# Sums of the norms by quarters of the tokens, roots on a quarter of the columns, and the heads' norms side by side

## What is computed

```python
def rmsnorm_3(x, g):
    x32 = x.astype(jnp.float32)
    y = x32 * lax.rsqrt(jnp.mean(x32 * x32, axis=-1, keepdims=True) + EPS)
    return (y * g.astype(jnp.float32)).astype(x.dtype)
...
    ml_out = jax.nn.sigmoid(ml_o.astype(f32)) * head_rmsnorm(ml_h, ml_norm_w, ML_HEADS)
```

## Time and profile before

| | |
|---|---|
| median of 3 runs | 3986.44 us (3984.21 to 3989.53) |
| the profiled execution | 3983.62 us, its span 3981.8 us, granted clock of PE 0.918 |
| PE busy | 3481.9 us (87%) |
| DVE, ACT, POOL busy | 1792.2, 1161.9, 974.5 us |
| norms | 20 of 512 columns, 4 of 264, 2 of 256, 1 of 16 |

### The profile page before, as it was taken

One profiled execution on the slowest core, in us unless ns is written; L12 is line 12 of the kernel. 1 busy time (PEld: TensorE's weight loads), 2 busy tenths in 40 slices (PEclk: granted clock), 3 DMA queues, 4 the chain that ended last, 5 costly groups with the idle time before them and its releaser, 6 DMA issues. The chain is left out here.

```text
span 3981.8 us, 40388 instructions
## 1 busy us (share of the span) xinstructions
PE 3481.9 (87%) x16055; PEld 2713.5 (68%) x16055; DVE 1792.2 (45%) x2748; ACT 1161.9 (29%) x1835; POOL 974.5 (24%) x414
## 2 busy tenths in 40 slices
PE   4999978998999799999897777799998835799998
PEld 3887735865888588888786653278887713467886
DVE  5994566654331323456207856522202088442211
ACT  2232323324442321121421133233223214443222
POOL 0001301432444122323220001034442300013443
PEclk8999988999999899999997778699998957699999
DMA  4222402451323123334210010022331200012332
GB/s 169 95 96 90 150 30 99 163 174 50 99 93 97 54 85 101 132 136 146 68 59 6 1 43 6 16 77 99 95 95 60 76 0 14 0 43 80 96 97 83
DMA packets 91047, 315.87 MB, mean 79 GB/s; under 512 B 10726, under 2 KB 12518, under 8 KB 89962
## 3 DMA queue, kind: packets, MB, share of 16 engines
q1 hardware_dynamic: 88492, 304.90, 23.4%
q10 hardware_dynamic: 2368, 8.39, 0.6%
HBM read 311.16 MB, written 2.10 MB: 79 GB/s over the span
## 5 line engine op out<-in xcount | busy, mean ns | idle before, releaser
L239 POOL TENSOR_TENSOR terms<-streams,terms 128x1024 fp32r<-128x1024 f32 (+2 forms) x410 | 974.3, 2377 | 2981.4 <-ACT terms L227 2981.4
L444 PE MATMUL bank<-terms,terms 128*128 128x512 f32 (+2 forms) x4096 | 1521.1, 371 | 127.3 <-DVE terms L650 58.5
L445 PE MATMUL bank<-terms,terms 128*128 128x512 f32 (+2 forms) x4096 | 1513.7, 370 | 0.0
L446 PE MATMUL bank<-terms,terms 128*128 128x512 f32 (+2 forms) x4096 | 1511.7, 369 | 0.0
L227 ACT ACTIVATE terms<-streams 128x1024 fp32r<-128x1024 f32 (+1 forms) x462 | 475.6, 1030 | 1818.6 <-PE bank L446 1658.6
L444 PEld LDWEIGHTS bank<-terms,terms 128*128 128x128 f32 x4096 | 780.1, 190 | 285.4 <-issue 133.4
L446 PEld LDWEIGHTS bank<-terms,terms 128*128 128x128 f32 x4096 | 780.5, 191 | 128.8
L445 PEld LDWEIGHTS bank<-terms,terms 128*128 128x128 f32 x4096 | 781.6, 191 | 122.8
L1403 DVE TENSOR_TENSOR stage<-stage,bank 128x256 f32<-128x256 f32 (+1 forms) x88 | 54.6, 622 | 598.6 <-ACT stage L1393 598.6
L910 DVE SCALAR_TENSOR_TENSOR arena<-arena,vec 128x512 f32<-128x512 f32 x240 | 162.5, 745 | 0.2
L598 PE MATMUL bank<-sq,mean 128*128 128x512 f32 (+2 forms) x226 | 108.0, 626 | 54.1 <-ACT sq L615 54.1
(11 more groups left out here) (290 smaller groups left out, 3190.7 us busy)
## 6 DMA issues: line engine op xcount, KB each, us to landing
streams<-in_ffn_w SPq DMA_DIRECT2D x104, 512.0 KB, 3.3
streams<-in_w_mod SPq DMA_DIRECT2D x72, 512.0 KB, 3.4
streams<-in_w_up SPq DMA_DIRECT2D x44, 512.0 KB, 3.2
streams<-in_w_gu SPq DMA_DIRECT2D x44, 512.0 KB, 3.5
streams<-in_w_ada SPq DMA_DIRECT2D x32, 512.0 KB, 3.3
streams<-in_w_down SPq DMA_DIRECT2D x32, 512.0 KB, 3.5
streams<-in_w_v SPq DMA_DIRECT2D x24, 512.0 KB, 3.9
streams<-in_ffn_w SPq DMA_DIRECT2D x24, 384.0 KB, 3.2
```

What stands on the lines that cost most here:

```text
L239: gp.tensor_tensor(self.low(m), self.raw(n), self.high(m), ALU.subtract).then_inc(self.low_made.sem, 1)
L444: pe.matmul(out, high[:, at], x_high, start=kk == start, stop=False)
L445: pe.matmul(out, high[:, at], x_low, start=False, stop=False)
L446: mm = pe.matmul(out, low[:, at], x_high, start=False, stop=kk == kts - 1)
```

## The change

The sum of a tile is taken by four matmuls in place of one (`by_strips`). Each has 32 columns of ones as weights and a quarter of the tokens as its moving side, and writes 32 partitions of the bank: quarter g of the tokens lies on partitions 32g to 32g+31, in the first 128 columns. The root and the reciprocal then work on 128x128. Behind the reciprocal, four matmuls of 128 columns (`widen`) with the matrices `k.strip` (one row of ones, row 32g, the rest zero) bring the quarters back to 128x512 in the same bank, and the products read PSUM instead of `k.rstd`. In a norm with a mean, ACT copies the quartered mean out of PSUM (`averages`), and `widen` spreads it before DVE subtracts. Norms of other widths go the same way with their own quarter (64, 66 or 4 columns).

`HeadNorms` replaces `stage_head_norms`: four heads in four banks and four parts of `k.rstd`, with the product with the gates taken beside. The first one stands inside the pass `MemoryStart` (gates, sums of the heads, first step of the queries, widening, second step), the second one between two `Halves` at the start of the next `run`. Two `run`s and two blocks with their barriers are gone.

```diff
-        self.ones = k.mean[:, mean, :]
+        self.ones = k.mean[:, mean, 0:32]
+        self.strip = n // 4
...
+    def by_strips(self, pe, of, x, start, stop):
+        w = self.strip
+        for g in range(4):
+            mm = pe.matmul(self.k.bank[of[0]][32 * g:32 * g + 32, :w], self.ones, x[:, g * w:(g + 1) * w],
+                           start=start, stop=stop)
+        return mm
+
+    def widen(self, pe, of, x):
+        w = self.strip
+        for g in range(4):
+            mm = pe.matmul(self.k.bank[of[0]][:, g * w:(g + 1) * w], self.k.strip[:, g, :], x, start=True, stop=True)
+        return mm
...
         if self.center:
             self.means_of(pe)
+            self.means_widened(pe)
         self.sums(pe)
+        self.widened(pe)
...
-            mm = pe.matmul(self.bank(self.mean_bank), self.ones, self.src(j), start=j == 0, stop=j == nt - 1)
+            mm = self.by_strips(pe, self.mean_bank, self.src(j), j == 0, j == nt - 1)
         mm.then_inc(k.pe_done.sem, 1)
+
+    def means_widened(self, pe):
+        k = self.k
+        pe.wait_ge(*k.averaged(1))
+        self.widen(pe, self.mean_bank, k.middle[:, :self.strip]).then_inc(k.spread.sem, 1)
...
             pe.wait_ge(*k.act_done(j + 1))
-            pe.matmul(self.bank(self.sum_bank), self.ones, self.squared(j), start=j == 0, stop=j == nt - 1
-                      ).then_inc(k.pe_done.sem, 1)
+            self.by_strips(pe, self.sum_bank, self.squared(j), j == 0, j == nt - 1).then_inc(k.pe_done.sem, 1)
+
+    def widened(self, pe):
+        k = self.k
+        pe.wait_ge(*k.inverted(1))
+        self.widen(pe, self.sum_bank, k.rstd[:, :self.strip]).then_inc(k.widened.sem, 1)
...
+    def averages(self, act):
+        k = self.k
+        act.wait_ge(*k.pe_done(1))
+        if k.spread.base:
+            act.wait_ge(*k.spread(0))
+        act.activation(k.middle[:, :self.strip], k.bank[self.mean_bank[0]][:, :self.strip], ACT.Copy
+                       ).then_inc(k.averaged.sem, 1)
...
-        if k.dve_done.base:
-            act.wait_ge(*k.dve_done(0))
-        act.activation(k.rstd[:, :self.n], self.bank(self.sum_bank), ACT.Sqrt, bias=self.eps
-                       ).then_inc(k.bank_free[self.sum_bank[0]].sem, 1)
+        if k.widened.base:
+            act.wait_ge(*k.widened(0))
+        act.activation(k.rstd[:, :w], k.bank[self.sum_bank[0]][:, :w], ACT.Sqrt, bias=self.eps
+                       ).then_inc(k.rooted.sem, 1)
...
-        dve.wait_ge(*k.pe_done(1))
+        dve.wait_ge(*k.spread(1))
...
+    def inverse(self, dve):
+        k, w = self.k, self.strip
+        dve.wait_ge(*k.rooted(1))
+        dve.reciprocal(k.rstd[:, :w], k.rstd[:, :w]).then_inc(k.inverted.sem, 1)
...
-        dve.wait_ge(k.bank_free[self.sum_bank[0]].sem, self.sum_bank[1] + 1)
-        dve.reciprocal(k.rstd[:, :n], k.rstd[:, :n]).then_inc(k.dve_done.sem, 1)
-        dve.wait_ge(*k.dve_done(self.centred + 1))
+        k, nt = self.k, self.nt
+        rstd = self.bank(self.sum_bank)
+        dve.wait_ge(*k.widened(1))
         for j in range(nt):
             x = self.whole(j) if self.center else self.src(j)
             if self.gain:
-                ins = dve.scalar_tensor_tensor(self.whole(j), x, self.gain(j), k.rstd[:, :n], ALU.mult, ALU.mult)
+                ins = dve.scalar_tensor_tensor(self.whole(j), x, self.gain(j), rstd, ALU.mult, ALU.mult)
...
+        dve.wait_ge(*k.dve_done(self.centred + nt))
+        dve.sem_inc(k.bank_free[self.sum_bank[0]].sem, 1)
...
+class HeadNorms(Pass):
...
+        self.banks = [k.take_bank() for _ in range(heads)]
...
+    def sums(self, pe):
+        k = self.k
+        for h, (b, uses) in enumerate(self.banks):
+            if uses:
+                pe.wait_ge(k.bank_free[b].sem, uses)
+            pe.wait_ge(*k.act_done(h + 1))
+            for g in range(4):
+                mm = pe.matmul(k.bank[b][32 * g:32 * g + 32, :P], k.mean[:, 2, 0:32],
+                               self.squares_at[:, h, g * P:(g + 1) * P], start=True, stop=True)
+            mm.then_inc(k.pe_done.sem, 1)
+
+    def widened(self, pe):
+        k = self.k
+        for h, (b, _) in enumerate(self.banks):
+            pe.wait_ge(*k.inverted(h + 1))
+            for g in range(4):
+                mm = pe.matmul(k.bank[b][:, g * P:(g + 1) * P], k.strip[:, g, :], k.rstd[:, h * P:(h + 1) * P],
+                               start=True, stop=True)
+            mm.then_inc(k.widened.sem, 1)
+
...
+    def roots(self, act):
+        k = self.k
+        if k.widened.base:
+            act.wait_ge(*k.widened(0))
+        for h, (b, _) in enumerate(self.banks):
+            act.wait_ge(*k.pe_done(h + 1))
+            act.activation(k.rstd[:, h * P:(h + 1) * P], k.bank[b][:, :P], ACT.Sqrt, bias=k.eps[:, 1:2]
+                           ).then_inc(k.rooted.sem, 1)
...
+    def inverses(self, dve):
+        k = self.k
+        for h in range(self.heads):
+            dve.wait_ge(*k.rooted(h + 1))
+            r = k.rstd[:, h * P:(h + 1) * P]
+            dve.reciprocal(r, r).then_inc(k.inverted.sem, 1)
...
+    def scaling(self, dve):
+        k = self.k
+        for h, (b, _) in enumerate(self.banks):
+            dve.wait_ge(*k.widened(h + 1))
+            dve.wait_ge(*k.dve_done(h + 1))
+            dve.scalar_tensor_tensor(self.out[:, h, :], self.out[:, h, :], k.v(self.weight, h), k.bank[b][:, :],
+                                     ALU.mult, ALU.mult).then_inc(k.dve_done.sem, 1)
+        for h, (b, _) in enumerate(self.banks):
+            dve.wait_ge(*k.dve_done(self.heads + h + 1))
+            dve.sem_inc(k.bank_free[b].sem, 1)
...
-        self.steps_of = {"pe": [("means", norm.means_of)] * norm.center + [("sums", norm.sums)],
-                         "act": [("squares", norm.squares), ("root", norm.root), ("shifted", norm.shifted)],
-                         "dve": [("centring", norm.centring)] * norm.center + [("scaling", norm.scaling)]}
+        mean = norm.center
+        self.steps_of = {"pe": [("means", norm.means_of), ("means", norm.means_widened)] * mean
+                         + [("sums", norm.sums), ("widened", norm.widened)],
+                         "act": [("means", norm.averages)] * mean
+                         + [("squares", norm.squares), ("root", norm.root), ("shifted", norm.shifted)],
+                         "dve": [("centring", norm.centring)] * mean
+                         + [("inverse", norm.inverse), ("scaling", norm.scaling)]}
...
+        dve.memset(k.strip[:, :, :], 0.0).then_inc(k.constants.sem, 1)
+        dve.wait_ge(*k.constants(5))
+        for g in range(4):
+            dve.memset(k.strip[32 * g:32 * g + 1, g, :], 1.0).then_inc(k.constants.sem, 1)
...
+        self.averages(act)
...
+    def tensor(self, pe):
+        self.gates.tensor(pe)
+        self.heads.sums(pe)
+        self.queries.tensor_step(pe, 0)
+        self.heads.widened(pe)
+        self.queries.tensor_step(pe, 1)
+
+    def scalar(self, act):
+        self.heads.squares(act)
+        self.gates.scalar(act)
+        self.heads.roots(act)
+        self.queries.scalar(act)

     def vector(self, dve):
-        dve.memset(self.k.arena[:, ML_QP:ML_Q], 0.0).then_inc(self.k.dve_done.sem, 1)
+        k, n = self.k, self.heads.heads
+        self.heads.gated(dve)
+        dve.wait_ge(*k.dve_done(n))
+        dve.memset(k.arena[:, ML_QP:ML_Q], 0.0).then_inc(k.more[3].sem, 1)
+        self.gates.vector(dve)
+        self.heads.inverses(dve)
+        self.queries.vector_step(dve, 0)
+        self.heads.scaling(dve)
+        self.queries.vector_step(dve, 1)
...
     passes = before + [SecondGains(k, 16, 0, 16, ((0, 0), (1, 1)), ()),
-                       Beside(k, down_one, ctx1, sums=4, squares=2, root=4, shifted=4, scaling=4), VectorsAgain(k, down_one)]
+                       Beside(k, down_one, ctx1, sums=4, squares=2, root=4, inverse=4, widened=5, shifted=5, scaling=5), VectorsAgain(k, down_one)]
...
-    passes.append(Beside(k, of_queries, ctx2, sums=3, squares=1, root=3, shifted=3, scaling=3))
+    passes.append(Beside(k, of_queries, ctx2, sums=3, squares=1, root=3, inverse=3, widened=4, shifted=4,
+                         scaling=4))
...
-    stage_head_norms(k, k.a(B2_OUT, 4, 512), "hg_norm", k.a(B2_QG + 4 * 512, 4, 512))
     run(k, memory_inputs(k, lat_src, src))
     stage_mlstm(k)
-    stage_head_norms(k, k.a(ML_OUT, 4, 512), "ml_norm", k.a(ML_O, 4, 512))
...
-    halves = Halves(k, lambda j: outs[j], h, DT)
+    first = Halves(k, lambda j: outs[j], h, HEADS2)
+    heads = HeadNorms(k, k.a(ML_OUT, HEADS2, 512), "ml_norm", k.a(ML_O, HEADS2, 512), HEADS2)
+    halves = Halves(k, lambda j: outs[HEADS2 + j], lambda j: h(HEADS2 + j), HEADS2, heads.ready)
...
-    meta = Beside(k, down, meta_norm(k), sums=4, squares=2, root=4, shifted=4, scaling=4)
+    meta = Beside(k, down, meta_norm(k), sums=4, squares=2, root=4, inverse=4, widened=5, shifted=5, scaling=5)
...
-    return [halves, out, third, up, LoadMeta(k), meta, final]
```

(15 more changed lines are left out.)

85 lines of the change are left out of this document (63 added, 22 removed).

## The result

The changed kernel takes 3880.26 us, the median of 4 runs (3876.61 to 3881.37), beside 3985.32 us of the kernel before in the same session: ratio 0.9731, 95% interval 0.972 to 0.9743. The profiled execution has a span of 3878.6 us, 103.2 less.

The account below looks back on a forecast made before the run. PE, busy 87% of the span, bounds the kernel, so time is won where it stands: 32.3 + 13.7 + 7.1 + 2.5 + 2.1 - 0.2 + 20.2 + 14.0 = 91.7 off 3983.62, plus 2.8: 3895 us, range 3880 to 3918.

Parts of the forecast that it names:

- PE's matmuls elsewhere are the same, so nothing gives it back later: Outside the changed stretches: PE's work stays the same, so the summed saving of 91.7 us stays whole.
- the amount added for the median of before: At the end of the sum: 2.8 us, by which the profiled execution before lay under its median of 3986.44.
- The clock rival: In the norms: PE's clock falls at each norm, so 17 widenings take 0.9 more: 15 us, 3910; chance 10%.
- RMS norms: Seven RMS norms of 512 columns: 12.08 us becomes 8.05 in three, others save 4.6 to 6.0; 32.3 saved in all.
- `ln2`: Norm with a mean: ACT's copy stands behind a Silu waiting for a DMA, centring starts 1.3 later; 2.1 us saved.
- Narrow norms and the rest: Norms of 256, 264 and 16 columns: small gains and losses, -0.2 us in all.
- The first heads' stretch: First heads' norms, from mixer through gates' layer to outputs' layer: 20.2 us saved, bounds 17 and 21.
- the 1.8 for a fast start: Gates' layer behind the first mixer: starting in the fast clock saves 1.8 us more.
- Pairs: Sums of the norms: strips run only two at a time, 0.53 us a tile, total 3906; chance 8%.
- strips one behind another: Sums of the norms: each strip waits for its weights, 1.0 us a tile, total 3964; chance 7%.
- The slower side: Sums of the norms: every one of eight records costs full length, 2.2 us a tile, total 4127; chance 3%.
- The gates' stretch: First heads' norms: PE stands at the heads' widening and scans come late, 10 us given back, 3905; chance 7%.

Follow-up runs that it names:

- e8: Changed kernel with the means' matmuls ordered quarter by quarter over all eight tiles, the sums of squares in their old order: 3898.77 us, ratio 0.978.
- e1: Changed kernel without HeadNorms at both places, heads' norms one behind another again, sums by quarters kept: 3922.49 us, ratio 0.9841.
- e2: Changed kernel with class Norm as before (one matmul a tile, 512 columns, no copy or widening), heads side by side kept: 3940.40 us, ratio 0.9886.
- e5: Kernel before, unchanged, for a second trace: 3985.25 us in one execution.
- e7: Kernel before with a block in which DVE clears 1536 columns ahead of the second mixer: 3983.75 us in one execution.
- e9: Changed kernel with unread matmuls: two ahead of and two behind a 512-column norm's sums, four strips behind each tile but the last: 3884.52 us, ratio 0.9741.
- e10: Changed kernel with the vectors' Silu and both waits for it moved behind ln2's root (ACT) and products (DVE): 3876.36 us, ratio 0.9727.
- e3: Changed kernel with the copy of the quartered mean made by DVE in place of ACT: 3882.14 us, ratio 0.9741.
- e4: Changed kernel with unread matmuls: four ahead of and five behind a 512-column norm's sums, one wide one behind each tile but the last: 3933.65 us, ratio 0.9875.
- e6: Kernel before with a block in which DVE clears 512 columns ahead of the second mixer: 3978.39 us in one execution.
- e11: Changed kernel with the edits of e9 and e10 together: 3874.83 us, ratio 0.9714.
- e12: Kernel before with the 512-column clearing block of e6 again, now timed over ten runs: 3975.86 us, ratio 0.9975.

## Why the prediction was wrong

**The bound and the mechanism held.** The time came from PE's stands at norms and heads' norms, and the prices of the single operations stand in the trace after: a tile by strips 0.24 (64 records in 1.95, forecast 0.27), squares 0.52 and 0.60, root 0.37, reciprocal 0.95, the widening 1.16 where the clock was fast (forecast 1.06). e8 shows that the strips really run side by side, e1 and e2 that the two parts are worth some 42 and 60 us with what the clock adds.

**The step that failed** is "PE's matmuls elsewhere are the same, so nothing gives it back later". It put the clock elsewhere at nothing: the same matmuls at another time may be granted another clock. The second mixer took 9.9 us less with the same 330 records, all of it in PE's busy time. It shows four lengths in fourteen traces, and each comes again to 0.1 us: 112.9 (before, e5, e8), 110.5 (e1, e7), 105.0 (e2, e9, e10), 103.0 (after, e3, e4, e6, e11, e12). The first negations already tell them apart: the third comes 21.75, 20.92, 21.69 and 21.34 us behind the first. Shift the kernel before by one short block and it gets the 103.0 of the changed one (e6, e12). Against such a kernel before, 3975.9 us, the change is worth 95.6 us, and 91.7 were summed. The range had no term for this, of either sign. Of the 14.7 us between 3895 and 3880.3 the stretches make 11.5, of which the mixer is 9.9; 2.8 are the amount added for the median of before, which had no counterpart after (profiled 3880.42, median 3880.26); the rest is rounding.

**The clock rival came true,** though the total does not show it. It had 10% and 15 us; 11 of 17 widenings ran slow, ten of them at 0.9 more, 10 us in all. The forecast counted on a fast clock because the sums of the earlier trace rows kept it; those sums filled PE, under the new ones it was busy 0.84 and 0.81 of the two stretches around the fall. e9, which fills their rounds, keeps 1.00 over the sums and takes the slow widening away in eight of the eleven places.

**Mis-sized terms.** RMS norms: 28.0 for 32.3; four of their seven widenings ran slow (3.7), the fast ones took 1.16 for 1.06, and the forecast's 8.05 is itself 0.14 too low in three of the norms, since 12.08 less 2.35, 0.32 and 2.40, with 1.06 and 0.12 added, is 8.19. `ln2`: the step "the copy stands on ACT behind the Silu" named only half; DVE's program waits for the same Silu (e3), and with the slow widening nothing was left of 2.1. Narrow norms and the rest: -0.2 became 6.5. The sums of the two context norms stand inside dense layers, on PE's own path, and these stretches are 1.5 and 2.3 shorter. The attention is 2.1 shorter: its four narrow norms became 1.2 longer (four widenings of 1.98 each), and the piece behind them went from 133.5 to 130.5 us, at a granted clock of 0.81 against 0.78. The other 0.6 is spread over places without an edit. The first heads' stretch: 21.7 for 20.2, just over its bound of 21. The gates' layer started at a granted clock of 0.50 as before, so the 1.8 for a fast start was not there; the outputs' layer and `w_out2` got such a start instead (1.4 and 1.8). PE was not made late by the heads' widening (0.9 expected), and the part ahead of the scans grew by 1.6 where 2.7 was expected. Without the mixer the terms sum to 93.4 for 91.7, since the slow widenings and these gains cancel.

**Range and rivals.** Pairs, and strips one behind another, are out (0.24 a tile). The slower side is out by the same number. The gates' stretch gave nothing back beyond its terms.

**Open:** what fixes the moments at which the chip lowers or raises the clock; the runs show only that in this mixer they repeat with the program and jump with a shift of 1 to 2 us. No run gave the changed kernel a slow mixer with nothing else altered; e8 has it with the means altered too.

## What to carry to other kernels

A stretch in which PE is nearly the bound, has short pauses and shows a mean granted clock between 0.5 and 1 may have several lengths, as this mixer has, and an edit ahead of it may throw it into another: give the forecast a term for it, and before you credit an edit with a gain, compare the untouched stretches one by one. A delay block in the kernel before is a cheap test. Sums over partitions of few distinct results are cheaper by column strips, if neighbours in PE's program use different strips and the shape of the weights changes seldom. When a norm gets lighter for PE, the matmul that ends it may run at half the clock.

## What the hardware showed that was not expected

The same mixer, same instructions, ran in 112.9, 110.5, 105.0 or 103.0 us, and a delay of about 1 us made the whole kernel 10 us faster (0.9975). A change between weights of 32 and of 128 columns cost about 0.14 us, an estimate from e4's rounds. Four matmuls on four column strips took the time of one (64 records in 1.95 us; 5.96 on the same strip in turn), and the granted clock fell to 0.50 within 2 us after the start of a norm's sums although PE worked in every 0.52 us round.
